# A twelfth 2 MB buffer in the ring of expert weights, with half the scratch of the dynamic DMAs

## The chip, the core and the metric

The kernel runs on one core of one Trainium2 chip. The metric is the device time of one execution in microseconds (us), as the median over runs. A profiled execution gives the trace from which all rows below are read.

## What is computed

Two layers over 512 tokens of 1024 channels. Each layer first mixes (one input projection, a causal depthwise convolution, a windowed attention, a spatial gate, one output projection, a layer norm), and then runs a mixture of 16 experts:

```python
def moe_ffn(x, w_router, router_bias, w_gate, w_up, w_down):
    ...
    gates = group_limited_router(x2d, w_router, router_bias)
    y = jnp.zeros((bsz * t, d), jnp.float32)
    for e in range(N_EXPERTS):
        he = jax.nn.silu(x2d @ w_gate[e]) * (x2d @ w_up[e])
        y = y + gates[:, e:e + 1] * (he @ w_down[e]).astype(jnp.float32)
```

The router gives each token two experts. An expert has 2 x 1024 x 512 weights for gate and up and 512 x 1024 for down, all in float32: 6 MB. A layer so reads 96 MB of expert weights, whatever the tokens choose.

## The kernel before

The tokens of an expert are put into chunks of 64 (at least one chunk for each expert). TensorE runs through the experts in order, and for each chunk does `widen` (L783, 64 matmuls in two halves), turns the hidden rows (L777), turns the next chunk's tokens (L771), and does `narrow` (L789, 16 matmuls). How many chunks an expert has is known only when the router is done; loops with bounds in registers run over them.

The weights of an expert are three **pieces** of 2 MB (16 KB in each of the 128 partitions): HIGH (gate and up, the upper half of the 1024 rows), LOW (the lower half) and DOWN. Piece number 3e + part, from 0 to 47, goes to buffer (3e + part) mod R of a ring of R buffers. R is 11 before. The buffers are memory that the mixing part of the layer uses for other things (`slot[r][n]`, which the profile calls w_gate, w_up and w_down; `xtok`, the token rows; `moew`, the low parts of the turned tokens), so the first R pieces of a layer are loaded one by one as those uses end. After that the queue of SyncE (SP) loads piece i when piece i - R has been read: `wide_half` of an expert's last chunk frees its HIGH piece, `wide_done` its LOW piece, `narrow_done` its DOWN piece. SP issues in the order in which it is written, and the hardware queue behind it moves the pieces in the order of their issue.

In the buffer `moex` lie before the change the high parts of the turned tokens (`xTh`, during mixing and for the router's logits), and during the experts four small tiles: `xgT` (the chunk's turned tokens), `heT`, `he` and `last_hot`.

GpSimd (POOL) fetches each chunk's token rows from DRAM two chunks ahead with an indirect DMA (`gather`, L1639), and adds each chunk's result to DRAM with another (`scatter`, L1633). VectorE moves a gathered chunk to where it is turned (`move_gathered`, L1432 and L1433); it does so for a layer's second chunk before it takes up the hidden rows of the first (L1419).

Ahead of a layer's experts stands the router: TensorE computes logits (L705 and L712, `lgT_done`), VectorE the choice, TensorE two tables (the second is `late_tables`, L759, `late_done`), and the first chunk's tokens are gathered by `first_tok`.

Of the kernel before, what the change touches and what calls it, by code (L numbers as in the profile page):

```python
# [28 lines left out]
P = 128  # L29
# [47 lines left out]
def build(nc, a):  # L77
    ctx = ExitStack()
    with ctx:
        def sem(name):  # L80
            return ctx.enter_context(nc.semaphore(name))


        def sb(name, shape, dt=F32):
            return ctx.enter_context(nc.sbuf_tensor(name, shape, dt))
# [4 lines left out]
        def shared(name, offset, cols, dt):  # L90
# [16 lines left out]
        xgT = moex[:, 0:512].rearrange("p (i h s) -> p i h s", i=4, h=2)  # L107
        heT = moex[:, 512:768].rearrange("p (k s) -> p k s", k=KF)
        last_hot = moex[:, 768:1792].rearrange("p (b j t) -> p b j t", b=2, j=TT)
        moemem = sb("moemem", [P, 2560])  # L110
# [3 lines left out]
        he = moex[:, 1792:2048]  # L114
# [105 lines left out]
        wexp_in = [sem(f"weights_in{r}") for r in range(11)]  # L220
# [46 lines left out]
        ring = [slot[2][2][:, :], slot[0][1][:, :], slot[0][2][:, :], slot[0][0][:, :],  # L267
                xtok[:, :, :].rearrange("p j n -> p (j n)"), moew[:, :],
                slot[1][0][:, :], slot[1][1][:, :], slot[1][2][:, :], slot[2][0][:, :], slot[2][1][:, :]]
# [34 lines left out]
        def _(sp):  # L304
# [35 lines left out]
            def load_rows(l):  # L340

                sp.wait_ge(wide_done, first_chunk(sp, l, E - 2) * 2)
                for j in range(TT):
                    sp.dma_start(ycomb[j], x1d[l][P * j:P * j + P, :]).then_inc(x1_in, 16)
# [8 lines left out]
            for l in range(DEPTH):  # L353
# [13 lines left out]
                else:  # L367

                    sp.dma_start(col[:, :], a["cols"][l]).then_inc(col_in, 16)
                    load_rows(l - 1)  # L370
# [19 lines left out]
                load_expert(l, 2, LOW_K)  # L390
                sp.wait_ge(gm_raw, 2 * (l + 1))
                sp.wait_ge(conv_norm, 2 * (l + 1))
                load_expert(l, 0, DOWN)
# [3 lines left out]
                load_expert(l, 0, LOW_K)  # L397

                sp.wait_ge(last_low, l + 1)
                sp.wait_ge(piece_low, (PIECES - 1) * (l + 1))  # L400
                load_expert(l, 2, HIGH_K)

                sp.wait_ge(op_half, TT * (l + 1))
                load_expert(l, 0, HIGH_K)

                sp.wait_ge(op_done, TT * (l + 1))
                load_expert(l, 3, HIGH_K)

                sp.wait_ge(ln_out, TT * (l + 1))
                load_expert(l, 1, HIGH_K)  # L410

                sp.wait_ge(x1_stored, 16 * TT * (l + 1))
                sp.wait_ge(tr_done, TT * (2 * l + 1))
                load_expert(l, 1, LOW_K)
                load_expert(l, 3, LOW_K)
# [10 lines left out]

                sp.wait_ge(narrow_done, starts[E - 3] * 2)
                sp.dma_start(rffn, a["rows_ffn"][l].partition_broadcast(P)).then_inc(rows_in, 16)
                if l + 1 == DEPTH:
                    load_rows(l)  # L430
# [1369 lines left out]
```

## Time and profile before

| | |
|---|---|
| median of 3 runs | 964.23 us (959.78 to 965.09) |
| profiled execution | 959.49 us, its span 957.7 us |
| PE busy (matmul) | 886.2 us, 93% of the span |
| DVE, POOL, ACT busy | 42%, 31%, 27% |
| DMA | 272.78 MB, mean 285 GB/s |

The span is what the trace covers; 1.8 us of the profiled execution lie around it. PE is TensorE. SPq is the queue of SyncE, where a row's duration is how long the issue of a transfer took: 0.37 us when the hardware queue has room, and as long as it takes until there is room otherwise. Busy time of PE counts overlapping matmuls once; whether it waits for weights is read from the waits and not from the busy share.

### The profile page before, as it was taken

How to read it: one execution, taken by the hardware profiler on the slowest of the kernel's cores; microseconds unless marked ns; L12 is line 12 of the kernel's file. 1: busy time of each engine (PE TensorE's matmuls, PEld its weight loads, DVE VectorE, ACT ScalarE, POOL GpSimd, SP SyncE). 2: the span in 40 equal slices, each digit the busy share in tenths (PEclk: the TensorE clock that was granted, in tenths of full speed). 3: DMA queues.
4: the chain of work that ended last, by engine and by line, in shares of the span. 5: the costliest groups of instructions: out<-in, count | busy, mean ns of one | idle time of the engine just before them, and what ended most of it. 6: DMA issues, size and time to landing. Idle time of an engine off the chain costs nothing.

```text
span 957.7 us, 15541 instructions
## 1 busy us (share of the span) xinstructions
PE 886.2 (93%) x5890; PEld 569.2 (59%) x5890; DVE 405.8 (42%) x928; ACT 253.8 (27%) x473; POOL 298.8 (31%) x220
## 2 busy tenths in 40 slices
PE   6999799789999997999999997997999999879995
PEld 5877678755555553555497776786555555435541
DVE  5997847721111111111659977368111111111126
ACT  5325741211111111111333357312111111111111
POOL 0632456232222222222335224661322222212213
PEclk9999899879999999999999998998899999999998
DMA  9851176889999999997414211769998999999962
GB/s 320 285 204 54 44 276 273 325 329 404 405 407 402 406 405 411 403 379 190 121 28 129 88 54 45 306 243 352 368 387 298 395 407 403 408 415 400 391 145 88
DMA packets 66133, 272.78 MB, mean 285 GB/s; under 512 B 8835, under 2 KB 24355, under 8 KB 40993
## 3 DMA queue, kind: packets, MB, share of 16 engines
q1 hardware_dynamic: 53792, 247.14, 65.1%
q0 software_dynamic: 12288, 24.89, 10.5%
q8 instruction: 40, 0.66, 0.3%
q14 instruction: 13, 0.10, 0.0%
HBM read 256.83 MB, written 21.76 MB: 291 GB/s over the span
## 4 chain that ended last, share of the span: by engine, by line
PE 65%; DVE 18%; DMA 10%; SPq 3%; issue 2%; ACT 1%; POOL 0%; DVEq 0%; POOLq 0%
PE bank L783 26%; PE bank L443 15%; PE bank L789 14%; DVE bank L1168 8%; DMA w_down<-in_exp_w_down 4%; DMA moew<-in_exp_w_down 4%; SPq L337 3%; PE bank L777 2%; DVE xTl L1137 2%; PE bank L771 2%; DMA moemem<-x_rows,first_tok 2%; PE bank L834 2%; PE bank L830 2%; DVE w_gate L1144 1%; DVE w_gate L1145 1%
## 5 line engine op out<-in xcount | busy, mean ns | idle before, releaser
L1419 DVE TENSOR_TENSOR moex<-bank,moemem 64x128 f32<-64x128 f32 x172 | 48.4, 281 | 330.6 <-ACT moemem L1046 327.9
L1639 POOL DMA_INDIRECT moemem<-x_rows,gather_idx x43 | 45.1, 1049 | 298.6 <-DVE moemem L1433 267.1
L1586 POOL TENSOR_TENSOR wl<-w_gate,wh 128x2048 fp32r<-128x2048 f32 x17 | 78.0, 4590 | 138.4 <-ACT wh L909 98.9
L443 PE MATMUL bank<-xTh,wh 128*128 128x512 f32 (+1 forms) x256 | 101.3, 396 | 11.4 <-DVE xTl L1137 10.0
L783 PE MATMUL bank<-w_up,moex 128*64 128x256 f32 x896 | 101.5, 379 | 1.9 <-DMA w_up<-in_exp_w_wide 1.9
L1046 ACT ACTIVATE moemem<-bank 64x256 f32<-64x256 f32 x86 | 32.8, 381 | 258.9 <-PE bank L783 258.9
L443 PE MATMUL bank<-xTh,wl 128*128 128x512 f32 (+1 forms) x256 | 95.5, 373 | 0.0
L443 PE MATMUL bank<-xTl,wh 128*128 128x512 f32 (+1 forms) x256 | 95.2, 372 | 0.0
L783 PE MATMUL bank<-w_gate,moex 128*64 128x256 f32 x768 | 87.1, 379 | 2.2 <-DMA w_gate<-in_exp_w_wide 2.2
L1633 POOL DMA_INDIRECT y_rows<-moemem,scatter_idx x43 | 69.3, 1612 | 62.6 <-ACT moemem L1051 57.3
L783 PEld LDWEIGHTS bank<-w_up,moex 128*64 128x64 f32 x896 | 64.2, 137 | 40.2 <-issue 7.4
L783 PE MATMUL bank<-w_down,moex 128*64 128x256 f32 x672 | 79.6, 391 | 0.6 <-DMA w_down<-in_exp_w_wide 0.6
L1168 DVE SCALAR_TENSOR_TENSOR bank<-w_down,col,bank 128x512 f32<-128x512 f32 x116 | 77.5, 747 | 1.4 <-DVE w_down L1152 0.5
L783 PEld LDWEIGHTS bank<-w_gate,moex 128*64 128x64 f32 x768 | 55.2, 137 | 38.0 <-issue 13.1
L1051 ACT ACTIVATE moemem<-bank,gatef 128x512 f32<-128x512 f32 x43 | 29.5, 687 | 159.2 <-PE bank L789 140.3
L783 PEld LDWEIGHTS bank<-w_down,moex 128*64 128x64 f32 x672 | 49.6, 142 | 29.5 <-issue 7.2
L443 PEld LDWEIGHTS bank<-xTh,wh 128*128 128x128 f32 x256 | 50.1, 196 | 22.6 <-issue 10.9
L1425 DVE COPY moex<-bank 128x128 f32<-128x128 f32 x86 | 25.1, 292 | 85.5 <-PE bank L777 85.5
L789 PE MATMUL bank<-w_down,moex 128*64 128x512 f32 x240 | 58.1, 605 | 1.9 <-DMA w_down<-in_exp_w_down 1.9
L443 PEld LDWEIGHTS bank<-xTh,wl 128*128 128x128 f32 x256 | 50.2, 196 | 10.2 <-issue 2.9
L443 PEld LDWEIGHTS bank<-xTl,wh 128*128 128x128 f32 x256 | 50.2, 196 | 8.2
L443 PE MATMUL bank<-wh,xTh 128*128 128x512 f32 x128 | 50.9, 397 | 2.8 <-DVE xTl L1137 2.8
(229 smaller groups left out, 1310.4 us busy)
## 6 DMA issues: line engine op xcount, KB each, us to landing
w_up<-in_exp_w_wide SPq DMA_DIRECT2D x20, 2048.0 KB, 24.0
w_gate<-in_exp_w_wide SPq DMA_DIRECT2D x18, 2048.0 KB, 32.8
w_down<-in_exp_w_wide SPq DMA_DIRECT2D x16, 2048.0 KB, 26.4
w_down<-in_exp_w_down SPq DMA_DIRECT2D x12, 2048.0 KB, 25.6
w_gate<-in_exp_w_down SPq DMA_DIRECT2D x8, 2048.0 KB, 17.8
w_gate<-in_w_in SPq DMA_DIRECT2D x13, 1024.0 KB, 5.8
xtok<-in_exp_w_wide SPq DMA_DIRECT2D x6, 2048.0 KB, 16.7
w_up<-in_exp_w_down SPq DMA_DIRECT2D x6, 2048.0 KB, 26.0
```

What stands on the lines that cost most here:

```text
L337: sp.dma_start(weights(e, part).rearrange("p (a b) n -> p a (b n)", b=2), src.rearrange("(a p b) n -> p a (b n)", p=P, b=2))\
L443: mm = pe.matmul(out, xs[i], ws[k], start=(first and n == 0), stop=(last and n == 2))
L783: return [pe.matmul(bank[i][CH * n:CH * n + CH, 0:256], x, w[:, 512 * n + 256 * i:512 * n + 256 * i + 256], start=(k == 0), stop=(k == KD ...
L789: return [pe.matmul(bank[5][CH * n:CH * n + CH, :], heT[:, k, :], wd[:, k, 512 * n:512 * n + 512], start=(k == 0), stop=(k == KF - 1)) for ...
L1046: act.activation(silu[:, 256 * i:256 * i + 256], bank[i][CH:P, 0:256], ACT.Silu).then_inc(silu_set, 1)
L1051: act.activation(ysb[b], bank[5][:, :], ACT.Copy, scale=gatef[:, bass.ds(c, 1)]).then_inc(y_set, 1)
L1168: y = dve.scalar_tensor_tensor(o, x, wk, o, ALU.mult, ALU.add)
L1419: dve.tensor_tensor(he[CH * b:CH * b + CH, P * i:P * i + P], bank[i][0:CH, P * b:P * b + P], silu[:, 256 * i + P * b:256 * i + P * b + P], ...
L1425: dve.tensor_copy(heT[:, 2 * i:2 * i + 2, :], bank[2 + i][:, 0:P].rearrange("p (k s) -> p k s", k=2))\
L1586: pool.tensor_tensor(wl[(n + l) % SLOTS][:, :], wraw[n % 2], wh[(n + l) % SLOTS][:, :].bitcast(F32), ALU.subtract)\
L1633: pool.indirect_dma_start(y_halves[l], bass.IndirectOffsetOnAxis(ap=scatter_idx[:, :], axis=0), ysb[0], None, bounds_check=2 * T - 1, oob_ ...
L1639: return pool.indirect_dma_start(to, None, x1_halves[l], bass.IndirectOffsetOnAxis(ap=rows[:, :], axis=0), bounds_check=2 * T - 1, oob_is_ ...
```

## The change

It makes `moex` whole a buffer of the ring, so R is 12. The four small tiles move from `moex` to `moemem`, which grows from 2560 to 4608 columns (8 KB more in each partition). These 8 KB come from the scratch in which the descriptors of POOL's dynamic DMAs lie, 8192 bytes in each partition instead of the default. The order of buffers in the ring is written anew, and with it which piece is loaded at which of the points where memory falls free. `load_rows` (the rows of the residual, 2 MB, for the end of the layer) waits for one expert less and stands for both layers right behind the last weight piece.

```diff
--- before.py
+++ after.py
@@ -104,14 +104,14 @@
         xtok = sb("xtok", [P, TT, D])
         xparts = [x[:, :].rearrange("p (k t) -> p k t", k=KD) for x in (xTh, xTl)]
 
-        xgT = moex[:, 0:512].rearrange("p (i h s) -> p i h s", i=4, h=2)
-        heT = moex[:, 512:768].rearrange("p (k s) -> p k s", k=KF)
-        last_hot = moex[:, 768:1792].rearrange("p (b j t) -> p b j t", b=2, j=TT)
-        moemem = sb("moemem", [P, 2560])
+        moemem = sb("moemem", [P, 4608])
         xg_next, xg = moemem[:, 0:512], moemem[:, 512:1024]
         ysb = [moemem[:, 1024:1536], moemem[:, 1536:2048]]
         silu = moemem[0:64, 2048:2560]
-        he = moex[:, 1792:2048]
+        xgT = moemem[:, 2560:3072].rearrange("p (i h s) -> p i h s", i=4, h=2)
+        heT = moemem[:, 3072:3328].rearrange("p (k s) -> p k s", k=KF)
+        last_hot = moemem[:, 3328:4352].rearrange("p (b j t) -> p b j t", b=2, j=TT)
+        he = moemem[:, 4352:4608]
 
         qr = slot[0][0][:, 0:2048].rearrange("p (m t) -> p m t", m=4)
         gv = slot[0][0][:, 2048:3072].rearrange("p (j c) -> p j c", j=TT)
@@ -217,7 +217,7 @@
         xtok_in, wr_in = sem("xtok_in"), sem("wr_in")
         wraw_in = [sem(f"wraw_in{i}") for i in range(2)]
         rows_in = sem("rows_in")
-        wexp_in = [sem(f"weights_in{r}") for r in range(11)]
+        wexp_in = [sem(f"weights_in{r}") for r in range(12)]
         dve_chain, pool_chain = sem("dve_chain"), sem("pool_chain")
         xT_high, xT_low = sem("xT_high"), sem("xT_low")
         head_in = [sem(f"head_in{i}") for i in range(4)]
@@ -264,9 +264,10 @@
 
         block = ctx.enter_context(nc.Block())
 
-        ring = [slot[2][2][:, :], slot[0][1][:, :], slot[0][2][:, :], slot[0][0][:, :],
-                xtok[:, :, :].rearrange("p j n -> p (j n)"), moew[:, :],
-                slot[1][0][:, :], slot[1][1][:, :], slot[1][2][:, :], slot[2][0][:, :], slot[2][1][:, :]]
+        ring = [slot[1][1][:, :], slot[1][0][:, :], slot[2][2][:, :],
+                xtok[:, :, :].rearrange("p j n -> p (j n)"), moex[:, :], slot[1][2][:, :],
+                slot[2][0][:, :], slot[2][1][:, :], moew[:, :],
+                slot[0][2][:, :], slot[0][1][:, :], slot[0][0][:, :]]
         R = len(ring)
         HIGH_K, LOW_K, DOWN = range(3)
 
@@ -339,7 +340,7 @@
 
             def load_rows(l):
 
-                sp.wait_ge(wide_done, first_chunk(sp, l, E - 2) * 2)
+                sp.wait_ge(wide_done, first_chunk(sp, l, E - 3) * 2)
                 for j in range(TT):
                     sp.dma_start(ycomb[j], x1d[l][P * j:P * j + P, :]).then_inc(x1_in, 16)
 
@@ -367,7 +368,6 @@
                 else:
 
                     sp.dma_start(col[:, :], a["cols"][l]).then_inc(col_in, 16)
-                    load_rows(l - 1)
                     load_piece(l, 0)
                     load_piece(l, 1)
                     mix_params(l)
@@ -387,32 +387,35 @@
                 sp.dma_start(rows3, a["rows_mix"][l].partition_broadcast(P)).then_inc(rows_in, 16)
 
                 sp.wait_ge(pt_done, TT * (l + 1))
-                load_expert(l, 2, LOW_K)
+                load_expert(l, 0, HIGH_K)
                 sp.wait_ge(gm_raw, 2 * (l + 1))
                 sp.wait_ge(conv_norm, 2 * (l + 1))
-                load_expert(l, 0, DOWN)
+                load_expert(l, 3, HIGH_K)
 
                 sp.wait_ge(conv_low, 2 * (l + 1))
                 sp.wait_ge(gm_low, 2 * (l + 1))
-                load_expert(l, 0, LOW_K)
+                load_expert(l, 3, LOW_K)
 
                 sp.wait_ge(last_low, l + 1)
                 sp.wait_ge(piece_low, (PIECES - 1) * (l + 1))
+                load_expert(l, 0, LOW_K)
+
+                sp.wait_ge(op_half, TT * (l + 1))
+                load_expert(l, 0, DOWN)
+
+                sp.wait_ge(op_done, TT * (l + 1))
                 load_expert(l, 2, HIGH_K)
 
-                sp.wait_ge(op_half, TT * (l + 1))
-                load_expert(l, 0, HIGH_K)
-
-                sp.wait_ge(op_done, TT * (l + 1))
-                load_expert(l, 3, HIGH_K)
-
                 sp.wait_ge(ln_out, TT * (l + 1))
-                load_expert(l, 1, HIGH_K)
+                load_expert(l, 3, DOWN)
 
                 sp.wait_ge(x1_stored, 16 * TT * (l + 1))
                 sp.wait_ge(tr_done, TT * (2 * l + 1))
+                load_expert(l, 1, HIGH_K)
+
+                sp.wait_ge(lgT_done, TT * (l + 1))
                 load_expert(l, 1, LOW_K)
-                load_expert(l, 3, LOW_K)
+                load_expert(l, 2, LOW_K)
 
                 sp.wait_ge(late_done, l + 1)
                 load_expert(l, 1, DOWN)
@@ -424,10 +427,9 @@
                     sp.wait_ge((wide_half, wide_done, narrow_done)[part], starts[e] * 2)
                     load_expert(l, i // 3, i % 3)
 
+                load_rows(l)
                 sp.wait_ge(narrow_done, starts[E - 3] * 2)
                 sp.dma_start(rffn, a["rows_ffn"][l].partition_broadcast(P)).then_inc(rows_in, 16)
-                if l + 1 == DEPTH:
-                    load_rows(l)
             for j in range(TT):
                 sp.wait_ge(row_set[j], DEPTH)
                 sp.dma_start(a["out"][P * j:P * j + P, :], xtok[:, j, :]).then_inc(out_stored, 16)
@@ -1790,7 +1792,7 @@
         "exp_w_wide": paired(np.concatenate([x["exp_w_up"], x["exp_w_gate"]], axis=3)),
         "exp_w_down": paired(x["exp_w_down"]),
     }
-    nc = bacc.Bacc("TRN2", target_bir_lowering=False, num_devices=1)
+    nc = bacc.Bacc("TRN2", target_bir_lowering=False, num_devices=1, dynamic_dma_scratch_size=8192)
     a = {n: nc.dram_tensor(f"in_{n}", v.shape, mybir.dt.from_np(v.dtype), kind="ExternalInput").ap()
          for n, v in arrays.items()}
     a["out"] = nc.dram_tensor("out_x", (T, D), F32, kind="ExternalOutput").ap()
```

The first place is SP's queue ahead of the experts, layer 0. The numbers behind w_gate, w_up and w_down are those of `slot`. Before:

```order
L337 DMA w_up1<-in_exp_w_wide 128x2x2048 [waits pt_done]
L337 DMA w_down0<-in_exp_w_down 128x2x2048 [waits conv_norm,gm_raw]
L337 DMA w_up0<-in_exp_w_wide 128x2x2048 [waits gm_low,conv_low]
L337 DMA w_gate1<-in_exp_w_wide 128x2x2048 [waits piece_low,last_low]
L337 DMA w_down2<-in_exp_w_wide 128x2x2048 [waits op_half]
L337 DMA w_gate2<-in_exp_w_wide 128x2x2048 [waits op_done]
L337 DMA w_gate0<-in_exp_w_wide 128x2x2048 [waits ln_out]
L337 DMA xtok<-in_exp_w_wide 128x2x2048 [waits tr_done,x1_stored]
L337 DMA w_up2<-in_exp_w_wide 128x2x2048
L337 DMA moew<-in_exp_w_down 128x2x2048 [waits late_done]
L337 DMA w_down1<-in_exp_w_down 128x2x2048
```

and of the change:

```order
L338 DMA w_up1<-in_exp_w_wide 128x2x2048 [waits pt_done]
L338 DMA w_down0<-in_exp_w_wide 128x2x2048 [waits conv_norm,gm_raw]
L338 DMA w_up0<-in_exp_w_wide 128x2x2048 [waits gm_low,conv_low]
L338 DMA w_gate1<-in_exp_w_wide 128x2x2048 [waits piece_low,last_low]
L338 DMA w_down2<-in_exp_w_down 128x2x2048 [waits op_half]
L338 DMA w_gate2<-in_exp_w_wide 128x2x2048 [waits op_done]
L338 DMA w_gate0<-in_exp_w_down 128x2x2048 [waits ln_out]
L338 DMA xtok<-in_exp_w_wide 128x2x2048 [waits tr_done,x1_stored]
L338 DMA moex<-in_exp_w_wide 128x2x2048 [waits lgT_done]
L338 DMA w_up2<-in_exp_w_wide 128x2x2048
L338 DMA w_down1<-in_exp_w_down 128x2x2048 [waits late_done]
L338 DMA moew<-in_exp_w_down 128x2x2048
```

The first eight points are the same, with the same buffers, but for the pieces they hold. At the point of `tr_done` and `x1_stored` stand two loads before, and three now, the second of which also waits for `lgT_done`. At `late_done` stand two, as before.

The second place is the start of the loop that follows on SP, where three loads, on wide_half, wide_done and narrow_done, follow one expert's reads: each waits until a piece of that expert has been read, and takes its buffer. Before:

```order
L337 DMA w_down2<-in_exp_w_down 128x2x2048 [waits wide_half]
L337 DMA w_up0<-in_exp_w_wide 128x2x2048 [waits wide_done]
L337 DMA w_down0<-in_exp_w_wide 128x2x2048 [waits narrow_done]
L424 REGISTER_ALU
L337 DMA w_gate0<-in_exp_w_down 128x2x2048 [waits wide_half]
L337 DMA xtok<-in_exp_w_wide 128x2x2048 [waits wide_done]
L337 DMA moew<-in_exp_w_wide 128x2x2048 [waits narrow_done]
L424 REGISTER_ALU
L337 DMA w_gate1<-in_exp_w_down 128x2x2048 [waits wide_half]
L337 DMA w_up1<-in_exp_w_wide 128x2x2048 [waits wide_done]
L337 DMA w_down1<-in_exp_w_wide 128x2x2048 [waits narrow_done]
```

and of the change:

```order
L338 DMA w_up1<-in_exp_w_wide 128x2x2048 [waits wide_half]
L338 DMA w_gate1<-in_exp_w_wide 128x2x2048 [waits wide_done]
L338 DMA w_down2<-in_exp_w_down 128x2x2048 [waits narrow_done]
L427 REGISTER_ALU
L338 DMA xtok<-in_exp_w_wide 128x2x2048 [waits wide_half]
L338 DMA moex<-in_exp_w_wide 128x2x2048 [waits wide_done]
L338 DMA w_down1<-in_exp_w_down 128x2x2048 [waits narrow_done]
L427 REGISTER_ALU
L338 DMA w_gate2<-in_exp_w_wide 128x2x2048 [waits wide_half]
L338 DMA w_up2<-in_exp_w_wide 128x2x2048 [waits wide_done]
L338 DMA moew<-in_exp_w_down 128x2x2048 [waits narrow_done]
```

Before, wide_half (a HIGH piece is free) lets a DOWN piece be loaded, since 11 is not a multiple of 3; now each kind of piece takes the place of its own kind, one whole piece further ahead.

The third place is the end of the loop on SP. Before:

```order
L337 DMA w_gate0<-in_exp_w_down 128x2x2048 [waits wide_half]
L427 REGISTER_ALU
L428 DMA w_down1<-in_rows_ffn 128x2048 [waits narrow_done]
L369 DMA col<-in_cols 128x106
L278 TENSOR_LOAD starti
L278 ISA x2
L342 REGISTER_ALU
L344 DMA w_up1<-x1_rows0 128x1024 [waits wide_done]
L344 DMA w_up1<-x1_rows0 128x1024 x3
L332 DMA w_gate1<-in_w_in 128x8x256 x2
```

and of the change:

```order
L338 DMA w_gate0<-in_exp_w_down 128x2x2048 [waits narrow_done]
L279 TENSOR_LOAD starti
L279 ISA x2
L343 REGISTER_ALU
L345 DMA w_up1<-x1_rows0 128x1024 [waits wide_done]
L345 DMA w_up1<-x1_rows0 128x1024 x3
L431 REGISTER_ALU
L432 DMA w_down1<-in_rows_ffn 128x2048 [waits narrow_done]
L370 DMA col<-in_cols 128x106
L333 DMA w_gate1<-in_w_in 128x8x256 x2
```

The four loads of token rows into w_up1 moved ahead of the rows of the second norm (`in_rows_ffn`) and of `col`.

## Rows read from the trace of the kernel before

**Rows 1.** PE's waits for DMAs: total us, times, longest.

```profile
PE bank L771 <- DMA moemem<-x_rows,first_tok: 6.7, 2, 3.8
PE bank L783 <- DMA xtok<-in_exp_w_wide: 3.5, 2, 1.9
...
PE bank L789 <- DMA moew<-in_exp_w_down: 3.3, 2, 1.8
...
PE bank L783 <- DMA w_gate<-in_exp_w_wide: 2.2, 2, 1.4
...
PE bank L783 <- DMA w_up<-in_exp_w_wide: 1.9, 1, 1.9
PE bank L789 <- DMA w_down<-in_exp_w_down: 1.9, 2, 1.5
...
PE bank L783 <- DMA w_down<-in_exp_w_wide: 0.6, 1, 0.6
```

**Rows 2.** Chain that ended last, layer 0: start us, us, what.

```profile
212.05 6.91 PE bank L783 x64
...
328.18 6.91 PE bank L783 x64
...
338.76 37.32 DMA moew<-in_exp_w_down
...
380.27 6.91 PE bank L783 x64
```

**Rows 3.** The same chain, layer 1.

```profile
816.57 6.91 PE bank L783 x64
...
853.14 38.13 DMA w_down<-in_exp_w_down
...
895.55 6.91 PE bank L783 x64
```

**Rows 4.** SP's queue around the router, layer 0: start us, us of issue.

```profile
183.75 0.37 SPq L337 DMA_DIRECT2D xtok<-in_exp_w_wide  x1
184.16 0.47 SPq L337 DMA_DIRECT2D w_up<-in_exp_w_wide  x1
199.17 0.37 SPq L337 DMA_DIRECT2D moew<-in_exp_w_down  x1
```

**Rows 5.** TensorE's last logits, layer 0: start us, us.

```profile
177.57 0.65 PE L712 MATMUL bank<-xTl,wrs 128*16 128x128 f32 x8
```

**Rows 6.** Busy time by stretch; last two: DMA busy share, GB/s.

```profile
196.00:202.00 6.00, 5.57 (x29) 4.29 (x30) 0.78 (x3) 0.60 (x1) 4.12 (x3) 0.55 0.47 110
673.00:677.00 4.00, 4.00 (x22) 2.94 (x22) 0.48 (x3) 0.60 (x1) 3.39 (x3) 0.50 0.59 139
722.00:729.00 7.00, 7.00 (x60) 4.13 (x58) 0.00 (x0) 0.77 (x2) 2.84 (x3) 1.00 0.35 66
206.00:423.00 217.00, 211.86 (x1569) 113.42 (x1567) 39.18 (x149) 37.57 (x75) 51.55 (x54) 1.00 1.02 405
730.00:905.00 175.00, 166.75 (x1224) 88.41 (x1222) 30.83 (x118) 29.64 (x58) 39.83 (x42) 1.00 1.02 405
```

**Rows 7.** SP's queue while it is full, layer 0.

```profile
320.53 5.83 SPq L337 DMA_DIRECT2D w_down<-in_exp_w_down  x1
...
389.64 5.16 SPq L337 DMA_DIRECT2D w_gate<-in_exp_w_down  x1
```

**Rows 8.** SP's queue in layer 1, at experts 1 and 2.

```profile
712.12 0.37 SPq L337 DMA_DIRECT2D moew<-in_exp_w_wide  x1
727.18 0.37 SPq L337 DMA_DIRECT2D w_gate<-in_exp_w_down  x1
```

**Rows 9.** POOL's second gather of each layer: start us, us.

```profile
195.84 1.06 POOL L1639 DMA_INDIRECT moemem<-x_rows,gather_idx  x1 [0.86 <-POOL gather_idx L1699]
...
672.50 1.05 POOL L1639 DMA_INDIRECT moemem<-x_rows,gather_idx  x1 [0.87 <-POOL gather_idx L1699]
```

**Rows 10.** VectorE: first hidden rows of each layer, and a gathered chunk's move.

```profile
206.11 0.60 DVE L1419 TENSOR_TENSOR moex<-bank,moemem 64x128 f32<-64x128 f32 x2 [4.23 <-ACT moemem L1046]
...
676.89 0.42 DVE L1433 COPY moemem<-moemem 128x512 f32<-128x512 f32 x1
682.88 0.60 DVE L1419 TENSOR_TENSOR moex<-bank,moemem 64x128 f32<-64x128 f32 x2 [5.57 <-ACT moemem L1046]
```

**Rows 11.** The gathers of line 1639 over the whole span: us from issue to landing.

```profile
DMA to landing us min/median/max: 7.5/8.1/8.6
```

**Rows 12.** The page's row of POOL's DMA queue: packets, MB, share.

```profile
q0 software_dynamic: 12288, 24.89, 10.5%
```

## The prediction

> **What bounds the kernel now.** I first looked at who waits for whom on PE. Nearly all the time of the experts is matmuls, and what PE waits for there is weights: the six lines with an expert piece sum to 3.5 + 3.3 + 2.2 + 1.9 + 1.9 + 0.6 = 13.4 us [rows 1]. The chain that ended last says what these waits cost. In layer 0 ten chunks start between 212.05 and 328.18, so a chunk takes 11.61 us. From 328.18 to 380.27 there are four chunks: 52.09 - 46.45 = 5.6 us too many, and the piece that ends the delay, a DOWN piece in moew, was issued at 338.76 and landed 37.3 us later [rows 2]. In layer 1 six chunks start between 816.57 and 895.55: 78.98 - 69.68 = 9.3 us too many, with a piece that needed 38.1 us [rows 3]. So the two layers' experts lose 14.9 us to late weights, the waits and a little around them.
>
> Next, why they are late. A transfer of 37 us is one that stood in a queue: SP issued a piece every (389.64 - 320.53) / 12 = 5.76 us there, since the queue was full [rows 7], and the DMA engines were busy all the time at 405 GB/s in both long stretches [rows 6]. An expert with one chunk eats three pieces in 11.6 us, the DMAs bring them in 17.3 us. PE lives on the lead that the DMAs had before, and in both layers that lead is used up by expert 12. A piece in that stretch comes earlier only if the DMAs were idle less before. So the view that decides is that of the stretches in which they rest although a piece could be moved [rows 6]:
> - layer 0, 196 to 202: 110 GB/s in place of 405, 6 x (1 - 110/405) = 4.4 us of transfer left out; by the busy share (0.47) it is 3.2 us. After it the stream doesn't stop before 423;
> - layer 1, 673 to 677: 4 x (1 - 139/405) = 2.6 us;
> - layer 1, 722 to 729: 7 x (1 - 66/405) = 5.9 us.
>
> The first two have one cause: two pieces were issued at 183.75 and 184.16, and nothing after them until `late_done` at 199.17 [rows 4]. The third is the ring being full: SP issued at 712.12, when expert 1 was through, and then had no free buffer until 727.18, when the HIGH piece of expert 2 had been read [rows 8]. Experts 1 and 2 of layer 1 have two chunks each, the time between these rows being one chunk and a half-wide part.
>
> **The change, part by part.**
>
> *A third piece behind x1_stored.* Its extra wait, `lgT_done`, costs nothing: the last logits of layer 0 start at 177.57 and take 0.65 us [rows 5], and SP comes there at 184. So three pieces are queued at about 184. The two of before kept the engines at work until some 196; the third takes 5 to 6 us more, to about 202, and the two of `late_done`, at 199.17, come before it is through. The rest at 196 to 202 is gone. All later pieces of layer 0 follow in a stream without a gap, so each lands earlier by what was filled: 3.2 us by the share, 4.4 by the bytes. I take 3.5, nearer to the share, since a piece is there only when the last of 16 engines has it, and that one rested less than the mean. The delay of 5.6 us shrinks by this, to 2.1.
>
> *The ring one piece deeper.* In layer 1 the piece issued at 727.18 is number 17, into the place of piece 6. With 12 buffers number 17 takes that of piece 5, free at 712.12, and it is number 18 that waits for 727.18 [rows 8]. The engines can do it: before, they had done number 16 by 722; they start the stretch 2.6 us earlier (the second rest is filled as in layer 0), so number 17 is through at about 722 + 5.7 - 2.6 = 725, before 727. From there each piece lands when its forerunner did: 5.7 us earlier, and the delay of 9.3 shrinks to 3.6. Bounds for a piece: 2.097 MB at 405 GB/s is 5.2 us, and SP's longest issue in the full queue is 5.8 [rows 6, 7]; the rest at 722 to 729 shrinks and doesn't vanish. The rest at 673 to 677 gives nothing of its own, since both kernels meet again at 727.18.
>
> The Trainium skill (DMA: Bandwidth & Descriptors, Bandwidth) says that for transfers from HBM to SBUF the HBM side binds at about 358 GB/s per core. The trace shows 405, so the measurement decides; by the page a piece would be an estimated 5.9 us, and the sum below 0.2 us larger.
>
> *The four small tiles in moemem, and which piece goes where.* The same instructions with the same shapes on each engine: 0. Pieces 3, 4 and 5 (expert 1), read from 212.05 on [rows 2], are now seventh, eighth and tenth in the order of loads, counted from 0: they land at about 191, 197 and 209 in layer 0, and the DOWN piece is read at 220. Piece 7 and piece 8 have some 12 us more.
>
> *load_rows earlier.* On SP it is behind the last weight piece as before, and ahead of `in_rows_ffn`, which comes 2 MB later, some 6 us, with 40 us to spare before the norm. `col` and the next layer's w_in are queued behind the same bytes. No wait of PE's is for any of them [rows 1]: 0.
>
> *Half the scratch.* POOL's queue moved 12288 packets, 768 for each of 16 engines, in an execution [rows 12]. POOL is free 69% of the time, and gathers two chunks ahead: a one-time stall below about 9 us stays hidden. 0.
>
> **Sum:** 3.5 + 5.7 = 9.2 us. From the profiled execution 959.49 to 950.3; its time lies 4.7 us below the median of the three, so against the median it is 964.23 - 9.2 = 955.0.
>
> **Rivals.**
> 1. *The second gather is late (slower).* It is issued at 195.84 and 672.50, in the rest that the change fills [rows 9]. In layer 1 it was there by 676.89, some 4 us later, and VectorE takes up the first chunk's hidden rows only after it has moved these rows, 0.42 us, at 206.11 and 682.88 [rows 10]. Among weights a gather takes 7.5 to 8.6 us [rows 11]: 195.84 + 8.6 + 0.6 = 205.0 and 672.50 + 8.6 + 0.6 = 681.7, still 1.1 and 1.2 us in time. So it decides from a latency of about 9.7 us, and each us above costs one in each layer: at 17 us it is 14.6, more than the gain, giving 969.6. If the gather had to wait for all that was queued ahead (a third piece) it could; but gathers land in 8.6 us at most in stretches where SP is 30 us ahead. 0.06. The Trainium skill (DMA: Bandwidth & Descriptors, Queues, rings and completion order) has each DMA engine take turns between the queues, packet by packet; by that rule the depth of SP's queue doesn't matter, and the trace agrees with 8.6 us.
> 2. *POOL stalls as its smaller ring fills.* Hidden up to 9 us; with two stalls of 8.6 us and no cover it would be 955.0 + 17.2 = 972. 0.02.
> 3. *Only the deeper ring pays.* The rest at 196 stays, because the engine that is last hadn't rested, or the third piece comes later: 964.2 - 5.7 = 958.5. 0.14.
> 4. *No change.* The stream is slower when fuller (the two long stretches then fall below 405 GB/s), or the delay is set by something that moves along: 964. 0.13.
> 5. *All delay goes.* The spread between DMA engines shrinks too, as they are less far behind: 964.2 - 14.9 = 949.3. 0.05.
>
> My forecast has 0.60. **Range:** 949 to 962 takes in rivals 3 and 5, and the run-to-run spread of 5 us; it leaves out the slower ones and most of no change. 0.5% is 4.8 us, about what a measurement of this kernel can tell: faster is the forecast, rival 5 and two thirds of rival 3 (0.75); the same is rival 4 and the rest (0.17); slower 0.08.
>
> **What would show it.** In layer 0 no rest of the DMAs between 196 and 202, and three issues near 184. In layer 1 pieces issued at about one per step at experts 1 and 2, with a rest of some 4 us left before 729. The waits of PE for weights sum to about 5 us in place of 13.4, still at expert 12 and in layer 1 up to expert 14. Expert stretches of 5.6 - 3.5 = 2.1 and 9.3 - 5.7 = 3.6 us over 11.61 a chunk. The second gather lands after some 8 us, with no wait of VectorE's behind it on the chain. It would be wrong if the long stretches fell below 405 GB/s, if L1419 of a first chunk came later, or if PE's waits moved to other pieces.

## The result, and the profile after

| | before | after |
|---|---|---|
| median of 4 runs each | 963.19 us (959.78 to 965.09) | 948.37 us (945.88 to 950.12) |
| profiled execution, its span | 959.49, 957.7 us | 945.88, 944.1 us |

The ratio is 0.9863, with a 95% interval from 0.9838 to 0.9887: 13.2 us faster, by between 10.9 and 15.6. (The two medians lie 14.8 us apart; with four executions of each, they tell the size no better than this interval.) Forecast were 9.2. The two profiled spans differ by 13.6 us.

Where PE waited for weights in the changed kernel (total us, times, longest); these answer to [rows 1]:

```profile
PE bank L773 <- DMA moemem<-x_rows,first_tok: 5.8, 2, 3.4
...
PE bank L791 <- DMA w_down<-in_exp_w_down: 1.8, 1, 1.8
...
PE bank L791 <- DMA moew<-in_exp_w_down: 1.2, 2, 0.8
PE bank L785 <- DMA w_gate<-in_exp_w_wide: 1.2, 1, 1.2
```

The three lines with a weight piece sum to 4.2 us in place of 13.4. The chain that ended last, layer 0 and then layer 1 (start us, us, what), answers to [rows 2, 3]; L785 is L783 of before:

```profile
340.97 6.91 PE bank L785 x64
...
369.27 37.65 DMA moew<-in_exp_w_down
411.10 6.91 PE bank L785 x64
...
799.18 6.91 PE bank L785 x64
...
841.62 38.72 DMA moew<-in_exp_w_down
884.61 6.91 PE bank L785 x64
```

At 11.613 us a chunk, six chunks in layer 0 take 69.68 us, and 70.13 pass: 0.5 too many, where there were 5.6. In layer 1 seven take 81.29, and 85.43 pass: 4.1 too many, where there were 9.3. I call this the **delay** below; it was measured in each run over all chunks behind a layer's first. It holds PE's waits and, where the matmuls behind a wait ran at half the clock, the time that this cost. The busy time by stretch (the last two columns are the DMAs' busy share and GB/s) answers to [rows 6]:

```profile
196.00:202.00 6.00, 4.57 (x22) 3.70 (x24) 1.24 (x3) 0.60 (x1) 4.48 (x4) 0.50 1.01 418
206.00:423.00 217.00, 216.62 (x1600) 115.69 (x1598) 40.06 (x152) 38.22 (x75) 53.74 (x57) 1.00 1.02 404
719.00:724.00 5.00, 5.00 (x50) 3.32 (x48) 0.41 (x2) 0.42 (x2) 1.61 (x1) 1.00 0.51 91
730.00:895.00 165.00, 161.21 (x1196) 86.56 (x1194) 29.53 (x112) 28.38 (x56) 38.60 (x40) 1.00 1.02 404
```

No rest is left at 196 to 202 (418 GB/s in place of 110). In layer 1 a rest is left, 5 us with 91 GB/s. Both long stretches stand at 404 GB/s (405 before).

The bytes say the same as the waits. Over the 105 us that end 5 us behind the start of layer 0's second chunk, the DMAs moved 290 GB/s before and 308 after: 1.9 MB more, which is 4.7 us at 405 GB/s. PE's waits for weights in layer 0 fall from 5.1 to 0.4 us, by the same 4.7.

SP's queue in layer 0 and at experts 1 and 2 of layer 1 answers to [rows 4, 8]:

```profile
185.47 0.37 SPq L338 DMA_DIRECT2D xtok<-in_exp_w_wide  x1
185.88 0.47 SPq L338 DMA_DIRECT2D moex<-in_exp_w_wide  x1
186.39 0.47 SPq L338 DMA_DIRECT2D w_up<-in_exp_w_wide  x1
200.18 0.37 SPq L338 DMA_DIRECT2D w_down<-in_exp_w_down  x1
200.59 0.47 SPq L338 DMA_DIRECT2D moew<-in_exp_w_down  x1
209.60 0.38 SPq L338 DMA_DIRECT2D w_up<-in_exp_w_wide  x1
...
706.34 0.37 SPq L338 DMA_DIRECT2D w_down<-in_exp_w_down  x1
721.41 0.37 SPq L338 DMA_DIRECT2D w_gate<-in_exp_w_wide  x1
```

Last, the end of the program. SP's waits there (total us, times, longest) and POOL's last instruction (ns, start us), of before:

```profile
SPq L79 <- PEq L79: 2.8, 1, 2.8
SPq L79 <- DMA out_x<-xtok: 2.5, 1, 2.5
L79 POOLq DRAIN  x1: 9692/9692/9692, 947.8 to 947.8; - x1
```

and of after:

```profile
SPq L79 <- DMA out_x<-xtok: 2.5, 1, 2.5
SPq L79 <- PEq L79: 0.2, 1, 0.2
L79 POOLq DRAIN  x1: 5606/5606/5606, 936.8 to 936.8; - x1
```

L79 is the line of the whole block, where all engines meet at the end. The wait is listed under PE, but PE was long done: before, POOL's DRAIN ran to 957.5, and SP came free then. After, it ends at 942.4, ahead of SP, which had its output stores in only at about 943.7. So the end is 2.6 us shorter. This was in no term of the forecast.

The 13.6 us of the two spans so are 5.2 (layer 0, delay 5.64 to 0.46), 5.2 (layer 1, 9.31 to 4.14), 2.6 (end), and 0.6 that belongs to stretches where nothing was changed: 3.4 us of matmuls at the half clock near 481 stand in the trace of before and not in that of after, worth some 1.5, and the first part of the program was 1.2 us slower the other way round (layer 0's second chunk starts at 212.05 before and at 213.22 after). Such stretches come and go between executions of one kernel: run 1 below, the kernel before once more, has no half clock near 481.

### The profile page after: what moved, and what is told of

Same layout as the page of the kernel before. It is cut to its first block, busy times and chain, and to the rows that moved or that the text cites. A ratio compares the mean times of both kernels' runs of the same rounds, so it can differ in the third digit from the quotient of the medians.

```text
span 944.1 us, 15539 instructions
## 1 busy us (share of the span) xinstructions
PE 883.0 (94%) x5890; PEld 567.4 (60%) x5890; DVE 407.5 (43%) x928; ACT 254.1 (27%) x473; POOL 298.5 (32%) x220
## 3 DMA queue, kind: packets, MB, share of 16 engines
q0 software_dynamic: 12288, 24.89, 10.6%
## 4 chain that ended last, share of the span: by engine, by line
PE 62%; DVE 16%; DMA 12%; SPq 5%; issue 2%; ACT 1%; POOL 1%; DVEq 0%; POOLq 0%
PE bank L785 25%; PE bank L791 14%; PE bank L445 13%; DMA moew<-in_exp_w_down 8%; DVE bank L1170 6%; SPq L338 4%; DMA w_gate<-in_w_in 2%; PE bank L779 2%; DVE xTl L1139 2%; PE bank L773 2%; PE bank L836 2%; DMA moemem<-x_rows,first_tok 2%; PE bank L832 2%; DVE w_gate L1146 1%; POOL wl L1588 1%
## 5 line engine op out<-in xcount | busy, mean ns | idle before, releaser
L1421 DVE TENSOR_TENSOR moemem<-bank,moemem 64x128 f32<-64x128 f32 x172 | 48.3, 281 | 312.5 <-ACT moemem L1048 309.8
L785 PE MATMUL bank<-w_up,moemem 128*64 128x256 f32 x1088 | 127.1, 388 | 0.0
L445 PE MATMUL bank<-xTh,wh 128*128 128x512 f32 (+1 forms) x256 | 100.1, 391 | 11.5 <-DVE xTl L1139 10.2
L785 PEld LDWEIGHTS bank<-w_up,moemem 128*64 128x64 f32 x1088 | 79.7, 140 | 45.1 <-issue 8.5
L785 PE MATMUL bank<-w_gate,moemem 128*64 128x256 f32 x736 | 83.4, 379 | 1.2 <-DMA w_gate<-in_exp_w_wide 1.2
L791 PE MATMUL bank<-w_down,moemem 128*64 128x512 f32 x320 | 77.5, 605 | 1.8 <-DMA w_down<-in_exp_w_down 1.8
L785 PEld LDWEIGHTS bank<-w_gate,moemem 128*64 128x64 f32 x736 | 52.7, 137 | 33.2 <-issue 6.8
L1427 DVE COPY moemem<-bank 128x128 f32<-128x128 f32 x86 | 25.1, 292 | 83.4 <-PE bank L779 83.4
L445 PEld LDWEIGHTS bank<-xTh,wl 128*128 128x128 f32 x256 | 49.2, 192 | 10.2 <-issue 2.9
L445 PE MATMUL bank<-wl,xTh 128*128 128x512 f32 x128 | 50.0, 390 | 0.0
L445 PE MATMUL bank<-wh,xTl 128*128 128x512 f32 x128 | 49.9, 390 | 0.0
```

The source lines that it names most:

```text
L445: mm = pe.matmul(out, xs[i], ws[k], start=(first and n == 0), stop=(last and n == 2))
L785: return [pe.matmul(bank[i][CH * n:CH * n + CH, 0:256], x, w[:, 512 * n + 256 * i:512 * n + 256 * i + 256], start=(k == 0), stop=(k == KD ...
L791: return [pe.matmul(bank[5][CH * n:CH * n + CH, :], heT[:, k, :], wd[:, k, 512 * n:512 * n + 512], start=(k == 0), stop=(k == KF - 1)) for ...
L1421: dve.tensor_tensor(he[CH * b:CH * b + CH, P * i:P * i + P], bank[i][0:CH, P * b:P * b + P], silu[:, 256 * i + P * b:256 * i + P * b + P], ...
L1427: dve.tensor_copy(heT[:, 2 * i:2 * i + 2, :], bank[2 + i][:, 0:P].rearrange("p (k s) -> p k s", k=2))\
```

## The experiments

All are compared with before, run on the same chip; the ratio has its 95% interval. The median of before beside them was 961.90 us for runs 1 to 4, 962.30 for 5 to 8, 961.34 for 9 and 10, and 963.28 for 11, so the ratios compare better than the medians do. Delay is per layer, waits are PE's for weights in both layers, end is SP's wait at the end; these four come from one profiled execution of each run.

| run | ratio | median us | delay, layer 0 | delay, layer 1 | waits | end |
|---|---|---|---|---|---|---|
| before | | 963.19 | 5.6 | 9.3 | 13.4 | 2.8 |
| 1 before again | 0.9982 (0.9965-0.9998) | 959.67 | 6.6 | 10.7 | 12.3 | 2.8 |
| 2 half scratch | 0.9959 (0.9943-0.9974) | 958.54 | 5.5 | 9.1 | 13.2 | 0.2 |
| 3 eleven early | 0.9942 (0.992-0.9965) | 956.97 | 5.5 | 10.2 | 11.6 | 0.2 |
| 4 twelve late | 0.9905 (0.988-0.9929) | 953.82 | 5.7 | 4.0 | 9.0 | 0.2 |
| 5 after again | 0.9862 (0.9832-0.9892) | 948.94 | 1.1 | 4.5 | 4.9 | 0.2 |
| 6 rows as before | 0.9881 (0.9851-0.9911) | 949.5 | 1.6 | 5.5 | 4.9 | 0.2 |
| 7 extra piece | 0.9958 (0.9937-0.9979) | 958.25 | 8.9 | 11.4 | 11.2 | 0.2 |
| 8 scratch 12288 | one execution | 961.89 | 5.4 | 11.0 | 13.2 | 0.8 |
| 9 eleven, bounds first | 0.993 (0.9908-0.9951) | 954.85 | 1.2 | 10.1 | 10.1 | 0.2 |
| 10 scratch 4096 | 0.9869 (0.984-0.9898) | 947.91 | 0.9 | 4.0 | 4.5 | 0.2 |
| 11 bounds first | 0.9873 (0.9843-0.9903) | 950.55 | 0.8 | 4.0 | 4.1 | 0.2 |

**1. Before, unchanged.** 

> The kernel before, unchanged, as a measure of what varies by itself. The changed kernel's profiled span was 13.6 us shorter, of which the experts' stretches hold 10.4 (5.2 in each layer); the rest is 1.5 us of half clock after layer 0's experts, 2.6 us in which SP waited for PE's end, and 1.3 us the other way in the first 70 us. Theory A, that these remainders are chance: this run shows other values for them (half clock there or not, end wait between 0.2 and 2.8 us), and a ratio of 1.000 within 0.3%. Theory B, that they belong to the kernel before: this run shows the half clock near 481 us and an end wait of 2.8 us again. Both expect delays by late weights of 5.6 and 9.3 us, within 0.5 us.

A program identical to before comes out at 0.9982, its interval just short of 1. Differences of 0.2% here say nothing. Its delays, 6.6 and 10.7 us against 5.6 and 9.3, tell how far those of one kernel stand apart; 3.4 us at the half clock behind a wait in layer 0 (370 to 380) are part of it.

**2. Before with half the scratch alone.**

```diff
+    nc = bacc.Bacc("TRN2", ..., num_devices=1, dynamic_dma_scratch_size=8192)
```

> The kernel before with only the scratch of the dynamic DMAs halved. My theory: nothing changes, ratio 1.000 within 0.3%, delays by late weights 5.6 and 9.3 us, gathers landing after 7.5 to 8.6 us. Rival, that the smaller ring of descriptors costs POOL something: POOL's DMA issues get longer than 1.05 and 1.6 us, or a gather is seen late, and the time goes up by 1 to 9 us. Rival, that a part of the gain comes from here (less traffic for descriptors): the pieces come faster than one in 5.76 us and the time goes down by 2 to 4 us.

POOL's DRAIN and SP's wait become those of after, to 10 ns, with the delays as they were:

```profile
SPq L79 <- PEq L79: 0.2, 1, 0.2
L79 POOLq DRAIN  x1: 5609/5609/5609, 949.0 to 949.0; - x1
```

The time falls by 3.9 us against before, and by 1.1 against run 1, which is the same as before: the measured times can only say that it falls by something between, the trace says 2.6. My theory, that nothing changes, was wrong. The time stands where a rival had put it, but not for that rival's reason: the pieces come no faster (406 and 405 GB/s in the long stretches).

**3. Eleven buffers, an earlier piece.** The small tiles are moved and the scratch is halved as in the change, `moex` takes the place of `moew` in the ring, and a third piece goes out ahead of `late_done`, so that one is left behind it:

```diff
-                xtok[:, :, :].rearrange("p j n -> p (j n)"), moew[:, :],
+                xtok[:, :, :].rearrange("p j n -> p (j n)"), moex[:, :],
...
                 load_expert(l, 1, LOW_K)
+
+                sp.wait_ge(lgT_done, TT * (l + 1))
+                load_expert(l, 1, DOWN)
                 load_expert(l, 3, LOW_K)
...
                 sp.wait_ge(late_done, l + 1)
-                load_expert(l, 1, DOWN)
                 load_expert(l, 2, DOWN)
```

> Eleven buffers as before, but moex takes the place of moew, so that three pieces are issued near 184 us and one at late_done. Alone: the early third piece. My theory: the rest of the DMAs at 196 to 202 us goes, and layer 0's delay falls from 5.6 us to about 0.4 as in the changed kernel; in layer 1 both meet again at the full ring, SP is without a free buffer until the HIGH piece of expert 2 is read (near 722), and the 9.3 us stay. Time 5 us below before, ratio 0.9946. Rival, that the deeper ring brings all: no change, 0 us. Rival, that the earlier stream carries into layer 1: 9 us or more.

Layer 0 did not give the 5 us that I expected. The stretch behind the filled rest, and SP's queue around it:

```profile
208.00:213.00 5.00, 5.00 (x28) 1.90 (x26) 1.54 (x6) 0.98 (x2) 0.73 (x1) 1.00 0.70 228
...
199.93 9.34 SPq L337 DMA_DIRECT2D w_down<-in_exp_w_down  x2
209.31 0.47 SPq L337 DMA_DIRECT2D w_up<-in_exp_w_wide  x1
```

There is a new rest at 208 to 213: 5 x (1 - 228/405) = 2.2 us. Behind `late_done` SP issues one piece (the row joins it with the next by its time), then reads 14 loop bounds into registers and issues nothing until about 208.8. One piece at `late_done` does not keep the DMAs at work over these 8 to 9 us; two do. The rest has moved, not gone. Of the delay of 5.5, the wait itself is 2.2 us; the remainder is matmuls at the half clock behind it (columns: start us, us):

```profile
374.16 1.97 PE L791 MATMUL bank<-moex,moemem 128*64 128x512 f32 x4 [2.23 <-DMA moex<-in_exp_w_down]
376.47 4.85 PE L791 MATMUL bank<-moex,moemem 128*64 128x512 f32 x12
...
388.87 1.08 PE L791 MATMUL bank<-moex,moemem 128*64 128x512 f32 x4
390.13 2.80 PE L791 MATMUL bank<-moex,moemem 128*64 128x512 f32 x12
```

The granted clock was 0.53 from 374 to 381. By the waits alone layer 0 gained 2.9 us (2.2 in place of 5.1), and the measured time fell by 5.6 (3.4 to 7.7), about what 2.9 and the end's 2.6 give; the half clock of one profiled execution can't be set against it. In layer 1, where the ring is no deeper than before, nothing is gained.

**4. The change with its third piece behind `late_done`.**

```diff
                 load_expert(l, 1, LOW_K)
-                load_expert(l, 2, LOW_K)
 
                 sp.wait_ge(late_done, l + 1)
                 load_expert(l, 1, DOWN)
+                load_expert(l, 2, LOW_K)
                 load_expert(l, 2, DOWN)
```

> The changed kernel, with the third load moved behind late_done, so that two pieces are issued near 184 us and three after 199. Alone: the deeper ring. My theory: the rest at 196 to 202 us is back and layer 0's delay is about 5 us again; layer 1's delay is 4.1 us as in the changed kernel, since its stream is set at expert 2. Time 5 us below before, ratio 0.9946, and 5 us above the changed kernel. Rival, that the deeper ring alone brings all: 10 us or more below before. Rival, that only the early piece counts: no gain.

In layer 0 the delay is back at 5.7 us, and in layer 1 it is 4.0, as with the change whole. So in the kernel with twelve buffers layer 0's gain hangs on the early piece, and layer 1's does not: there the depth is enough. Run 4 has its second rest too, at 677 to 681, and loses nothing by it, as forecast. The median stands 4.9 us above run 5's, by the ratios it is 4.1, and the delays differ by 4.2.

The size in layer 0 is not wholly accounted for. The rest that comes back is a smaller one than in before, 179 GB/s from 201 to 205, which is 2.2 us by its bytes. The two pieces ahead of it were also issued 1.2 us later, measured against the second chunk. Over the 105 us of above the DMAs moved 295 GB/s, 3.4 us less than the change's 308, and the waits are 5.3 in place of 0.4 us: 1.5 us more than the bytes explain.

**5. The change, unchanged.** 

> The changed kernel, unchanged. The runs so far leave this sum: 10.4 us from earlier weights, and 2.6 us from the end of the program, where POOL's last DRAIN takes 5.6 us with half the scratch and 9.7 us with the whole. My theory: delays by late weights of 0.5 and 4.1 us within 0.5, a DRAIN of 5.6 us, and 13 us below before, ratio 0.9865 within 0.002. Rival, that the first comparison was lucky and the gain is the 10.4 us of weights alone: ratio 0.989 or above, or other delays.

It repeats: 0.9862. Its delays (1.1 and 4.5) give gains of 4.6 and 4.8 us against before's trace, where the first pair gave 5.2 and 5.2. Better than any pair are the means. Before and runs 1, 2 and 8, whose weights go the old way, have 5.8 and 10.0 us; after and runs 5, 6, 10 and 11 have 1.0 and 4.4. That is a gain of 4.8 us in layer 0 and of 5.6 in layer 1.

**6. The change with `load_rows` where it stood before.**

```diff
-                sp.wait_ge(wide_done, first_chunk(sp, l, E - 3) * 2)
+                sp.wait_ge(wide_done, first_chunk(sp, l, E - 2) * 2)
...
+                    load_rows(l - 1)
                     load_piece(l, 0)
...
-                load_rows(l)
                 sp.wait_ge(narrow_done, starts[E - 3] * 2)
...
+                if l + 1 == DEPTH:
+                    load_rows(l)
```

> The changed kernel, with the loads of the residual rows back where they were (layer 0: behind the norm's rows and the columns; one expert later). My theory: no change against the changed kernel, within 0.2%, delays 0.5 and 4.1 us. Rival, that the earlier place is worth something: the end of a layer starts later, or VectorE or POOL waits for rows, 1 to 3 us.

949.5 against 948.9, 0.9881 against 0.9862, with intervals that overlap over most of their length: the edit is worth nothing that can be told from the spread, which leaves room for 1 or 2 us.

**7. The change with a thirteenth transfer of 2 MB, which nothing reads, behind the two of `late_done`.** It computes the same, and moves 4 MB more in an execution.

```diff
                 load_expert(l, 2, DOWN)
+                extra_piece(l)
```

> The changed kernel with one more transfer of 2 MB in each layer (DRAM to DRAM, read by nobody), issued behind the pieces of late_done. My theory, that the lead of the stream sets the time: in layer 0 every later piece lands 5.7 us later, and the delay grows from 0.5 to about 6.2; in layer 1 the rest that is left before expert 2's release takes up some 4 of the 5.7 us, and the delay grows from 4.1 to about 6. Sum 7 to 8 us above the changed kernel. Rival, that the stream has slack: nothing. Rival, that nothing sets it anew in layer 1: 11 us.

One transfer too many ahead of the stream costs 9.3 us by the medians. The waits for weights rise from 0.4 to 5.1 us in layer 0, about one piece's time, and from 3.8 to 6.1 in layer 1, as expected. The other 2.3 of the 9.3 were not expected; layer 0 shows what they can be, a wait and then matmuls at the half clock:

```profile
364.99 1.08 PE L800 MATMUL bank<-w_gate,moemem 128*64 128x512 f32 x4 [1.73 <-DMA w_gate<-in_exp_w_down]
366.26 4.49 PE L800 MATMUL bank<-w_gate,moemem 128*64 128x512 f32 x12
...
366.00:371.00 5.00, 5.00 (x19) 1.74 (x19) 0.78 (x3) 0.00 (x0) 1.25 (x2) 0.66 1.02 431
```

The granted clock over these 5 us is 0.66, a mean of 2.4 and 1.2 GHz, and over 383 to 388, behind the next wait, it is 0.66 again. The profiled execution, 964.91 us, is the longest of the ten, so its half clock (6.8 us in layer 0, 10.2 in layer 1) is more than the others had.

**8. Before with a scratch of 12288 bytes (measured once), and 10. the change with 4096.** 

> The kernel before with 12288 bytes of scratch, three quarters. POOL's last DRAIN took 9.69 us with 16384 and 5.61 with 8192. If its length goes with the size of the scratch, it takes 7.65 us here, and SP waits about 0.6 us for POOL at the end. If it has two values, 5.6 or 9.7. The delays by late weights stay 5.6 and 9.3 within 1.5 us.

> The changed kernel with 4096 bytes of scratch. From 9.69, 7.60 and 5.60 us at 16384, 12288 and 8192 bytes, POOL's last DRAIN should take some 3.6 us. It gains nothing, since SP's wait for the output's stores ends last already at 5.6 us (POOL is waited for 0.2 us): ratio that of the changed kernel within 0.002, delays by late weights 0.5 to 1.1 and 4.1 to 4.5. Rival, that a still smaller ring makes POOL wait for descriptors: gathers and scatters issued later, a DMA issue above 1.1 or 1.7 us, and a longer time.

POOL's DRAIN follows the size, in run 8 and in run 10:

```profile
L79 POOLq DRAIN  x1: 7603/7603/7603, 952.0 to 952.0; - x1
```

```profile
L79 POOLq DRAIN  x1: 4180/4180/4180, 937.3 to 937.3; - x1
```

With 9.69 and 5.61 us at the default and at 8192, that is 2.0 to 2.1 us for 4096 bytes, and 1.4 for the last. SP waits 2.8, 0.8, 0.2 and 0.2 us: from 8192 down the output stores end last, and a shorter DRAIN is worth nothing (0.9869 against 0.9862).

**9. Run 3 with the loop bounds read ahead of `late_done`, and 11. the same edit on the change.**

```diff
+                sp.wait_ge(start_set, l + 1)
+                starts = [first_chunk(sp, l, e) for e in range(1, E - 1)]
                 sp.wait_ge(late_done, l + 1)
...
-                starts = [first_chunk(sp, l, e) for e in range(1, E - 1)]
```

> The kernel with eleven buffers and the early third piece, and one edit more: SP reads the experts' loop bounds before it waits for late_done, not after. There SP could issue nothing for some 9 us after the last piece of late_done, the DMAs rested again at 209 to 212 us, and 2.2 us of waits for weights were left in layer 0 (and 3.3 us of half clock behind them). My theory: the deeper ring covers just this in layer 0, so with the bounds read early the rest at 208 to 213 us goes (above 400 GB/s in place of 228), and PE's waits for weights in layer 0 fall from 2.2 us to below 0.7; layer 1 keeps 9 to 11 us of delay. Time 1 to 5 us below the run without this edit. Rival, that the depth acts in layer 0 in another way: the 2.2 us of waits stay.

> The changed kernel with the loop bounds read by SP before it waits for late_done, as a version that might beat both. My theory: with twelve buffers the two pieces of late_done keep the DMAs at work until SP issues again at 209.6, so there is no rest to fill (above 400 GB/s from 206 to 213 us with and without the edit), and layer 1 is set at expert 2: no change, ratio 0.9865 within 0.002, delays 0.5 to 1.1 and 4.1 to 4.5 us. Rival, that pieces issued at 203 in place of 209 help (the wait is for each piece and not for the stream): layer 0's last 0.4 to 1 us of waits goes.

The stretch at 208 to 213 in run 9, against 228 GB/s in run 3:

```profile
208.00:213.00 5.00, 5.00 (x28) 1.92 (x26) 1.06 (x5) 0.98 (x2) 0.56 (x1) 1.00 1.02 415
```

The rest is gone, and layer 0's delay with it: 1.2 us with eleven buffers, with waits of 1.1 (0.7 was expected). That is the change's own layer 0. The measured time shows less of it: 0.993 against run 3's 0.9942 is 1.2 us, with intervals that overlap, at the lower end of the 1 to 5 expected; of the 4.2 us between the two delays, 3.3 are no waits in run 3's trace.

What the reads themselves cost is seen in SP's queue on the change, run 11:

```profile
199.26 0.47 SPq L338 DMA_DIRECT2D moew<-in_exp_w_down  x1
204.42 0.37 SPq L338 DMA_DIRECT2D w_up<-in_exp_w_wide  x1
```

With the bounds read beforehand the next piece goes out 4.7 us behind the last one of `late_done`, and these are a wait for PE, which has still to read the HIGH piece of expert 0. In the change it goes out 8.5 us behind. So of these 8.5 us the reads account for 3.8; the first 4.7 SP would have waited in any case. On the change the edit finds no rest to remove (414 GB/s at 206 to 213 with it, 413 without) and gives nothing. No kernel tried is measurably faster than the change.

## Why the prediction was right, and where it was not

*The third piece behind x1_stored: right, mis-sized.* Three issues stand at 185 to 186, and the rest is filled. The term was 3.5 us, and it measured 5.2 (4.6 in run 5, and 4.8 between the means). I had two readings of the same rest, 3.2 by busy share and 4.4 by bytes, and took one nearer to the smaller on the argument that the last of the 16 engines had rested less than the mean. Nothing in the runs bears this out. With the 418 GB/s that the stretch now reaches, bytes give 6 x (418 - 110)/405 = 4.6 us. Of the two readings the bytes were the one to take here.

*What I did not see there* is that SP issues nothing for over 8 us behind `late_done`, before and after: at first because it reads loop bounds, at the end only because of that (run 11). The forecast held because two pieces stand queued at that point; run 3 shows that with one it would not have, and run 9 that this was the reason. The deeper ring so does a second thing, which I had put down to layer 1 alone: it lets three pieces go early and two still cover the reading of the bounds. That layer 0 came out as forecast was luck in this respect.

*The ring one piece deeper: right.* Forecast 5.7, measured 5.2 (4.8 in run 5, and 5.6 between the means). The step is visible as I had put it: number 17 goes out at 706.34 where number 16 went at 712.12, both 5.8 us earlier than in [rows 8] as the layer starts earlier, and number 18 waits for the HIGH piece of expert 2, at 721.41. Of the rest some 4 us were to remain: 5 x (1 - 91/404) = 3.9. (It begins earlier, at 717; from 717 to 724, at 120 GB/s, it is 4.9.) Run 4 has this gain alone, its layer 1 being 4.0.

*Tiles, order of pieces, `load_rows` at 0: nothing speaks against it.* Run 6 shows it for `load_rows`, to within 1 or 2 us. For the tiles and the new order no run stands by itself. Run 9 comes out as the change does in layer 0 with the old order, which leaves nothing for the order there; the tiles lie in `moemem` in both.

*Half the scratch at 0: wrong.* I had asked only whether POOL would stall in its stream, and that it did not. The price stood at the end of the program, where POOL's DRAIN was the last thing that SP waited for, 2.8 us. The row was in the trace of before; I had not followed the chain to its last instruction. Runs 2, 8 and 10 show the cause. 5.2 + 5.2 + 2.6 = 13.0 us against the 13.2 of the ratio, and so do the means, 4.8 + 5.6 + 2.6. Of the 4 us that the forecast of 9.2 lacked, 2.6 are this term.

*Rivals.* The second gather did not come late, and layer 1 was as near to it as the 1.2 us I had worked out from 8.6 us. POOL issues it and VectorE moves it and takes up the hidden rows:

```profile
666.92 1.05 POOL L1641 DMA_INDIRECT moemem<-x_rows,gather_idx  x1 [0.87 <-POOL gather_idx L1701]
...
675.33 0.15 DVE L1434 COPY gather_idx<-toki 128x1 int32 x1 [6.21 <-DMA moemem<-x_rows,gather_idx]
675.40 0.42 DVE L1435 COPY moemem<-moemem 128x512 f32<-128x512 f32 x1
677.10 0.60 DVE L1421 TENSOR_TENSOR moemem<-bank,moemem 64x128 f32<-64x128 f32 x2 [1.29 <-ACT moemem L1048]
```

VectorE has the rows 8.4 us behind the start of their issue, with 1.3 us to spare before 677.10. By itself this gather doesn't tell whether it waited for what was queued: of the three pieces issued at 655.57 to 656.49 at most 4.1 MB had been moved when it was issued (361 GB/s over 11.35 us), so that some 2.2 MB, 5.4 us, were ahead of it. All 43 gathers of the execution tell it: they landed in 3.9 to 8.3 us, while pieces on SP's queue took up to 38.7. So a gather does not wait for SP's queue. The Trainium skill (DMA: Bandwidth & Descriptors, Queues, rings and completion order) says that a DMA engine serves its queues in turn, packet by packet; the trace agrees with 8.3 us at most. Rival 2, POOL stalls, did not come: its issues of gathers and scatters take 1.05 and 1.61 us with the whole scratch, with half, and with a quarter of it (run 10). Rival 3, only the deeper ring pays, is what run 4 built: 953.8, and the change is 4.9 below it (4.1 by the ratios). Rival 4, a slower stream, is refuted: both long stretches stand at 404 GB/s, and the 1 below 405 is worth 0.5 us over 217 at most. Rival 5, all delay goes, came true in layer 0 alone, nearly. Its 949.3 us is the number nearest to the measured 948.4, and that is chance: 4.1 us of delay are left in layer 1, and the end gave 2.6.

*The range.* The median of 948.4 lies 0.6 us below its lower end. The scratch's 2.6 us are what it lacked. The ratio, taken of the 964.2 that the forecast set out from, gives 951.0, which is inside.

*Still open.* The 1.5 us of waits in run 4's layer 0 that its bytes do not explain. The 5.7 us of delay there sit beside waits of only 5.3, and the change's 4.1 in layer 1 beside 3.8; the small remainder was not followed. Why the half clock follows one wait of 2 us and not another isn't settled either.

## What to carry to other kernels

When a queue of transfers runs without a gap for hundreds of us and its reader ends by waiting, look at the rests far ahead of the wait: in this kernel each byte left out there was paid for at the end (1.9 MB, 4.7 us), by the bytes and not by the busy share. Before you count on a rest being filled, look at what the issuing engine does next; a queue that must last over its register reads needs more than one piece. And follow the chain to the last instruction of the program: what each engine does when it is told to stop can be on the path, and a size that seems to belong to memory alone can set it.

## What the runs showed of the chip

- GpSimd's last DRAIN grows with the scratch for dynamic DMAs: 4.18, 5.61, 7.60 and 9.69 us at 4096, 8192, 12288 and the default's 16384 bytes (8192 being half of it).
- Reading 14 loop bounds takes SP over 8 us (the change issues nothing between 200.59 and 209.60). With the reads elsewhere (run 11) its next piece went out 5.2 us behind the one before, in place of 9.0.
- A wait of PE's for weights of some 2 us is in some places followed by 3.4 or 6.8 us at 1.2 GHz (the granted clock is 0.66 over 5 us in run 7), which costs 1.7 or 3.4 us, about as much again as the wait or more. Removing a wait so gives more than its length, now and then.
- One program, run 12 times and 23 times under two names on one chip, came out 0.18% apart.
